# Building the slot table of a mixture of experts with one-hot products, and streaming the next layer's modulation through router and dispatch

## The reference, cut to what matters

```python
scores = sigmoid(hf @ router_w)                       # 512 x 64
# 4 of 8 groups are kept, then 6 experts of each token
top_w  = take(scores, top_idx); top_w = top_w / sum(top_w) * 2.5
# slot table: every expert owns a run of slots; slot_tok[slot] = token (or none)
out    = swiglu(h_pad[slot_tok], w_gate[e], w_up[e], w_down[e])
routed = sum over the 6 picks of  out * top_w
x      = x + gt2 * (routed + swiglu(hf, shared weights))
# next layer: shift, scale, gate = split(silu(c) @ w_mod + b_mod)
```

## Time and profile before

| | us |
|---|---|
| median of 3 runs | 3005.1 (2999.84 to 3009.19) |
| the profiled execution, its own time | 3002.39 |
| its span in the trace | 3000.7 |
| mean granted TensorE clock | 0.921 of full speed |
| busy: PE, DVE, ACT, POOL | 2539.4, 1357.8, 708.0, 480.1 |

### The profile page before, as it was taken

One profiled execution on the slowest core, in us unless ns is written; L12 is line 12 of the kernel. 1 busy time (PEld: TensorE's weight loads), 2 busy tenths in 40 slices (PEclk: granted clock), 3 DMA queues, 4 the chain that ended last, 5 costly groups with the idle time before them and its releaser, 6 DMA issues. The chain is left out here.

```text
span 3000.7 us, 48849 instructions
## 1 busy us (share of the span) xinstructions
PE 2539.4 (85%) x19595; PEld 1484.2 (49%) x19595; DVE 1357.8 (45%) x2706; ACT 708.0 (24%) x1319; POOL 480.1 (16%) x449
## 2 busy tenths in 40 slices
PE   5999864986599999994679999979998498989988
PEld 2553444945244434331235556458887135545553
DVE  1550646525211111113588795966665562034442
ACT  3111440112011111110324551023333113134441
POOL 0000132300311111110100000022211220025450
PEclk8999877997799999997799999989999799999999
DMA  6110610012599999995715555244443932021001
GB/s 252 45 56 2 225 22 16 7 56 103 164 382 389 391 411 406 393 390 206 255 58 143 161 146 174 109 130 125 133 124 84 351 115 93 6 37 21 15 29 63
DMA packets 329700, 471.39 MB, mean 157 GB/s; under 512 B 152223, under 2 KB 225875, under 8 KB 304773
## 3 DMA queue, kind: packets, MB, share of 16 engines
q1 hardware_dynamic: 302645, 373.86, 36.4%
q10 hardware_dynamic: 12960, 69.21, 5.7%
q0 software_dynamic: 13872, 25.21, 2.3%
HBM read 413.73 MB, written 76.60 MB: 163 GB/s over the span
## 5 line engine op out<-in xcount | busy, mean ns | idle before, releaser
L1871 PE MATMUL psum<-ex_w,hT 128*64 128x512 f32 (+1 forms) x1104 | 333.0, 624 | 24.6 <-DMA ex_w<-in_exp_w_up 22.9
L1871 PEld LDWEIGHTS psum<-ex_w,hT 128*64 128x64 f32 (+1 forms) x1104 | 125.5, 160 | 226.0 <-issue 223.8
L3961 POOL TENSOR_SCALAR mla_pool<-mla_pool,at_stats 128x768 f32<-128x768 f32 x64 | 140.2, 2203 | 254.9 <-DVE at_stats L3979 254.9
L2107 DVE COPY slot_act_t<-psum 128x256 f32<-128x256 f32 x45 | 19.1, 424 | 326.8 <-PE psum L1879 326.8
L557 PE MATMUL psum<-hT,weights 128*128 128x512 f32 x384 | 166.8, 592 | 0.0
L1887 PE MATMUL psum<-ex_w,slot_act_t 128*64 128x512 f32 (+1 forms) x552 | 163.4, 597 | 1.4 <-DVE slot_act_t L2107 1.4
L1856 POOL DMA_INDIRECT scratch_ys<-slot_out,slot_row x45 | 45.5, 1011 | 467.3 <-issue 405.0
L557 PEld LDWEIGHTS psum<-hT,weights 128*128 128x128 f32 x384 | 73.0, 190 | 86.7 <-issue 86.1
L2063 ACT ACTIVATE slot_silu<-psum 128x256 f32<-128x256 f32 x45 | 17.2, 383 | 399.5 <-PE psum L1871 399.5
L3135 PE MATMUL psum<-rs_r_ident,rs_b 64*32 64x96 f32 x1536 | 84.3, 249 | 17.9 <-POOL rs_k_ident L3107 16.5
L3859 PE MATMUL psum<-mla_kT,at_qT 128*128 128x512 f32 (+1 forms) x256 | 93.3, 489 | 2.6 <-DVE at_qT L3971 1.6
(11 more groups left out here) (560 smaller groups left out, 4983.0 us busy)
## 6 DMA issues: line engine op xcount, KB each, us to landing
ex_w<-in_exp_w_gate SPq DMA_DIRECT2D x64, 1024.0 KB, 9.6
ex_w<-in_exp_w_up SPq DMA_DIRECT2D x64, 1024.0 KB, 19.4
ex_w<-in_exp_w_down ACTq DMA_DIRECT2D x60, 1024.0 KB, 10.0
mod_ring<-in_w_mod SPq DMA_DIRECT2D x12, 2048.0 KB, 13.2
scratch_features<-tokens SPq DMA_DIRECT2D x96, 256.0 KB, 3.8
weights<-in_w_in SPq DMA_DIRECT2D x6, 2048.0 KB, 8.1
ex_w<-scratch_ys SPq DMA_DIRECT2D x8, 1536.0 KB, 15.4
ex_w<-in_mod_w SPq DMA_DIRECT2D x6, 2048.0 KB, 20.7
```

Of the source, the lines that this page charges most:

```text
L1871: mm = pe.matmul(bank[at:at + n, :], XT[:, k, at:at + n], W[:, 0:2, k * DE:(k + 1) * DE], start=(k == 0), stop=(k == KD - 1))
L3961: pool.tensor_scalar(Pm[:, q % 2, u, :], Pm[:, q % 2, u, :], st[:, 3, u:u + 1], None, ALU.mult)\
```

## The change

The scatters, the table in HBM, its fill and its read back go. In `dispatch`, after each pick's slot is known, DVE splits the slot into tile and position and writes two one-hot (or scaled one-hot) arrays: `at_pos` (token x 128 positions, for 4 groups of tokens in one instruction) and `at_tile` (token x 69 tiles, with the token's number plus one as value, four instructions). PE multiplies them, 24 products summed in one bank, which is the table already transposed; empty slots are zero. The products stand in PE's list between the two halves of the shared expert's gate and up. The first three gathers of rows move from `all_experts` into `dispatch` behind the index lists; the row buffers are kept over both phases, are used for the token rows first, and are zeroed by POOL.

The modulation stream moves out of `combine`: vectors, bias rows and the first weight chunk are requested in `norm_turn`, chunks 0 to 2 run in `router`, 3 to 5 in `dispatch`. Its ring lies in the buffers of the first resident experts, so these are loaded later, and in the order 0, 2, 1. In `dispatch` DVE now takes the index lists first and after them, in this order, the modulation's columns, the shared expert's two products and the list of further experts. `combine` has no modulation left on any engine. It loads all rows into buffers of their own, in eight loads, each with its semaphore. Semaphores are cleared in ranges.

```diff
 def phase(nc, names, before=None, later=None):
...
-                    for h in handles:
-                        sp.sem_clear(h)
+                for a, b in zip(starts, ends):
+                    sp.sem_clear(range(a, b + 1))
 def load_router(I, sp, R, rw, bias, steps):
...
-    for w in range(3):
-        sp.dma_start(Wb[:, 0, w, :]..., shared[w]...).then_inc(R["sh_in"], 16)
+    sp.dma_start(steps[:, :, :], I["consts"][:, IOTA_COL:ALL_COLS]...).then_inc(R["in_done"], 16)
 class NextMods:
+    def request(self, I, sp):
+        vectors_in(sp, I, self.vec, self.H["vec_in"])
+        self.M.load_bias(sp)
+        self.M.load(sp, 0)
 def router(...):
         @block.sync
+            for n in range(1, RING):
+                M.load(sp, n)
+            for w in range(3):
+                sp.dma_start(Wb[:, 0, w, :]..., shared[w]...).then_inc(S["sh_in"], 16)
+            sp.wait_ge(S["in_done"], 48)
         @block.tensor
...
             mm.then_inc(S["mm_done"], 1)
+            pe.wait_ge(S["mod_silu"], 1)
+            for n in range(RING):
+                M.part(pe, n)
+                if n:
+                    M.sum(pe, n - 1)
+            M.sum(pe, RING - 1)
         @block.scalar
+            act.activation(mods.silu[:, :, 0:2], ..., ACT.Silu).then_inc(S["mod_silu"], 1)
...
+            for n in range(RING):
+                M.evac(act, n)
+                if n:
+                    M.to_row(act, n - 1)
+            M.to_row(act, RING - 1)
 def dispatch(...):
         @block.tensor
             mm.then_inc(S["pos_mm"], 1)
+            M.part(pe, RING)
             pe.wait_ge(S["beaten"], 1)
...
+            for n in range(RING + 1, M.N):
+                M.part(pe, n)
+                M.sum(pe, n - 1)
+            M.sum(pe, M.N - 1)
             for j in range(JX):
...
                 .then_inc(S["order_mm"], 1)
+            pe.wait_ge(S["m_row"], M.N)
+            columns_mm(pe, K, K.bank[0], M.row, (0, D)).then_inc(S["c_mm"], 1)
+            pe.wait_ge(S["sh_in"], 48)
             for m in range(2):
                 if m:
+                    for u in range(TOP_K * JX):
+                        pe.wait_ge(S["picked"], 2 * (u // JX) + 2)
+                        mm = pe.matmul(K.bank[1][:, 0:TILES], at_pos[:, u, :], at_tile[:, u, :],
+                                       start=(u == 0), stop=(u == TOP_K * JX - 1))
+                    mm.then_inc(S["idx_mm"], 1)
...
-            pe.wait_ge(S["back"], 16)
-            pe.transpose(K.bank[1][:, 0:TILES], back[:, :], ...).then_inc(S["idx_mm"], 1)
         @block.scalar
+            M.evac(act, RING)
+            for n in range(RING + 1, M.N):
+                M.evac(act, n)
+                M.to_row(act, n - 1)
+            M.to_row(act, M.N - 1)
             for j in range(JX):
         @block.sync
-            sp.dma_start(table, fill[:, :]).then_inc(S["filled"], 16)
+            for n in range(RING, M.N):
+                M.load(sp, n)
+            sp.wait_ge(S["m_row"], M.N)
+            sp.dma_start(gate_rows, M.row[0:2, 2 * D:3 * D]).then_inc(S["g_stored"], 16)
...
-            for q in range(RESIDENT):
-                load_expert(sp, Wb, buffer_of(q), src(expert_at(sp, order, q)), S["ex_in"])
-            sp.wait_ge(S["scattered"], 1)
-            sp.dma_start(back[:, :], table).then_inc(S["back"], 16)
+            sp.wait_ge(S["c_mm"], 1)
+            sp.wait_ge(S["g_stored"], 16)
+            for q in (0, 2, 1):
+                e = src(expert_at(sp, order, q))
+                if q == 1:
+                    sp.wait_ge(S["idx_mm"], 1)
+                load_expert(sp, Wb, buffer_of(q), e, S["ex_in"])
         @block.gpsimd
-            for k in range(TOP_K):
-                for j in range(JX):
...
-                    pool.indirect_dma_start(
-                        out=slot_tokens, out_offset=..., in_=K.const[:, TOKEN_COL + u:TOKEN_COL + u + 1], ...)
...
+            for n in range(RING, M.N):
+                M.add_bias_of(pool, n)
+            for n in range(2):
+                pool.wait_ge(S[f"h_st{n}"], 32)
+            pool.memset(Hg[:, :, :], 0.0).then_inc(S["zeroed"], 1)
+            pool.wait_ge(S["idx_out"], 1)
+            for t in range(RING_H):
+                gather_rows(pool, Hg[:, t, :], idx[:, first_column(t):...], h_rows, S[f"got{t}"])
         @block.vector
+            dve.wait_ge(S["m_part"], M.N)
             for k in range(TOP_K):
...
-                step.put(dve.tensor_reduce(to_f[:, k, :], pr[:, :, :], AX.X, ALU.add))
+                step(dve.tensor_reduce(to_f[:, k, :], pr[:, :, :], AX.X, ALU.add))
+                step.put(dve.tensor_scalar(tile0[:, k, :], to_f[:, k, :], ...))
...
+                step.put(dve.tensor_scalar(tile0[:, k, :], tile0[:, k, :], WHOLE, None, ALU.add))
...
+                step(dve.tensor_scalar(tile0[:, k, :], tile0[:, k, :], -WHOLE, float(SLOTS), ALU.add, ALU.mult))
+                step(dve.tensor_tensor(in_tile[:, k, :], to_f[:, k, :], tile0[:, k, :], ALU.subtract))
+                dve.tensor_tensor(at_pos[:, k * JX:(k + 1) * JX, :], ..., ALU.is_equal).then_inc(S["picked"], 1)
+                for j in range(JX):
+                    ins = dve.tensor_scalar(at_tile[:, k * JX + j, :], steps[:, 1, 0:TILES], tile0[:, k, j:j + 1],
+                                            number[:, k, j:j + 1], ALU.is_equal, ALU.mult)
+                ins.then_inc(S["picked"], 1)
...
+            columns_out(dve, K.bank[0], ..., next_mods[:, 1, :, :], next_mods[:, 0, :, :], S["c_out"])
+            for n in range(2):
...
+                dve.tensor_tensor(aT[:, n, :], sg[:, :], K.bank[up_bank[n][1]][:, :], ALU.mult).then_inc(S["act_done"], 1)
...
 def all_experts(...):
-            pool.wait_ge(S["zeroed"], 1)
-            for t in range(RING_H):
-                gather(t)
-            dve.memset(Hg[:, :, :], 0.0).then_inc(S["zeroed"], 1)
 def combine(...):
-            vectors_in(sp, I, vec, S["vec_in"])
-            load(0)
-            load(1)
...
-            for n in range(3):
-                M.load(sp, n)
-            M.load_bias(sp)
...
+            for n, (j, h) in enumerate(LOADS):
+                k = slice(h * TOP_K // 2, (h + 1) * TOP_K // 2)
+                sp.dma_start(rows[:, j, k, :], ys...).then_inc(S[f"in{n}"], 16)
+                if n == 1:
+                    sp.dma_start(gb[:, :], I["g_final"].partition_broadcast(P)).then_inc(S["g_in"], 16)
+            sp.dma_start(K.X[:, 0:JC, :], I["ctx_2"][0]...).then_inc(S["ctx_in"], 16)
...
-            M.evac(act, 0)
-            for n in range(M.N):
...
+            for j in range(JX):
+                lengths(j)
+                if j:
+                    next_lengths(j - 1)
```

More of the change, by code:

```diff
@@ L52, in phase @@
 @contextmanager
-def phase(nc, names, before=None):
+def phase(nc, names, before=None, later=None):
     with ExitStack() as own:
         by_name = {n: own.enter_context(nc.semaphore(n)) for n in names.split()}
-        signals = {**by_name, **(before or {})}
-        handles = list(signals.values())
+        cleared = {**by_name, **(before or {})}
+        handles = list(cleared.values())
+        signals = {**cleared, **(later or {})}
         with nc.Block(no_gpsimd_drain=True) as block:
@@ L65, in _ @@
                 nums = sorted(h.num for h in handles)
-                if nums[-1] - nums[0] + 1 == len(nums):
-                    sp.sem_clear(range(nums[0], nums[-1] + 1))
-                else:
-                    for h in handles:
-                        sp.sem_clear(h)
+                starts = [n for n in nums if n - 1 not in nums]
+                ends = [n for n in nums if n + 1 not in nums]
+                for a, b in zip(starts, ends):
+                    sp.sem_clear(range(a, b + 1))
 class Chain:
@@ L156, in constants @@
     out[:, LANE_COL:FUTURE_COL] = np.triu(np.ones((RC, RC)), 1).reshape(1, -1)
+    out[:, IOTA_COL:IOTA_COL + P] = np.arange(P)
+    out[:, IOTA_COL + P:ALL_COLS] = np.arange(P) * SLOTS
     e = np.arange(RC + 1)[None, :]
@@ L2413, in mixture @@
         Wb = sb("ex_w", [P, AT_ONCE, 3, KD * DE])
+        Hg, steps = sb("slot_rows", [P, RING_H, D]), sb("slot_steps", [P, 2, P])
+        G = held(nc, c, GATHERED)
         spare = K.hT[:, :, :].rearrange("p k t -> p (k t)")
@@ L2417, in mixture, with ahead @@
             rw, bias = sb("rt_w", [P, KD, NE], F32, c2), sb("rt_bias", [P, NE], F32, c2)
-            R = held(nc, c2, "in_done sh_in")
+            R = held(nc, c2, "in_done")
+            mods = NextMods(K, I, Wb, held(nc, c, NextMods.SEMS))
+            def ahead(sp):
+                load_router(I, sp, R, rw, bias, steps)
+                mods.request(I, sp)
             norm_turn(K, range(JC, NT), K.mods[:, 1, 0, :, :], K.mods[:, 1, 1, :, :], K.inv,
-                      ahead=lambda sp: load_router(I, sp, R, rw, bias, Wb, shared))
-            router(K, I, wt, kept, R, rw, bias)
-        dispatch(K, wt, kept, slot_of, w_of, extra, order, h_rows, slot_tokens, idx, to_row, Wb, src, acc)
```

(6 more changed lines are left out.)

231 lines of the change are left out of this document (104 added, 127 removed).

## The result

The changed kernel takes 2964.1 us (median of 4 runs, 2958.97 to 2970.11); the kernel before took 3005.1 beside it. The ratio is 0.9863, 95% interval 0.9846 to 0.988.

What follows compares the result with a forecast made beforehand. PE and DMA were taken to bound the experts, waits router, dispatch and combine; +16.2 up to the first pass and -31.9 in combine made -15.7, 2986.7 or 2989.4 by base, forecast 2988 us, range 2974 to 3001.

Steps and rivals of the forecast that it cites:

- Fewer clears of semaphores: At changes of phase: clears hidden or gone, below 4.43 us, between 0 and -1, taken as 0.
- Dispatch, first pass +16.2 us: Router and dispatch up to the first expert pass: PE turns the first rows at 831.1 instead of 814.85.
- Ranks to order: In dispatch: ranks and chunk 3's part end at 747.4, chunks 4 and 5 at 758.6, order at 764.9.
- Picks: DVE in dispatch: six picks of 4.4 us each, 2.17 before, ending at 791.6; bounds 3.5 and 5.5 a pick.
- Sum: Whole kernel: +16.2 - 31.9 = -15.7 us; bounds picks -0 to +5, products -3 to +2, combine's tail -2 to +4, cold starts -5 to 0.
- Combine: Combine stage: 57.5 us instead of 89.4, so -31.9, bound by DVE, its first sum 6 us in.
- the stall that I had named: In dispatch: DVE is through with its slots at 755 and stands until 764.9 for the order.
- Late lists: Rival, 18%: dispatch's chunk loads land 5 us later and each pick takes 5.5, so +5 and +4, 2997 us.
- a load-bound combine: Rival, 8%: DVE waits about 3 us at each combine tile, 12 us of the gain go, 3000 us.
- a PE stuck at the low level: Rival, 6%: PE in dispatch stays at the low clock, about +44 us, 3032 us.
- The clock holds: Rival, 12%: parts, both halves and products run at the high clock, 11.4 us less, about 2977 us.
- a product like these doesn't raise the clock: PE in dispatch: the 24 products leave the clock low; 8 us taken, between 4.9 at high clock and 9.7.

Runs made afterwards that it cites:

- experiment 1: Kernel before with range clears (283 fewer): 2991.03 us, ratio 0.9952; changed kernel with single clears: 2988.59 us; kernel before with single clears doubled: 3026.7 us.
- experiment 3: The changed kernel with POOL's zeroing of the gather block moved behind the index lists, away from DVE's picks: 2961.59 us, ratio 0.9854.
- experiment 4: The changed kernel with POOL's zeroing behind the index lists and the order product right behind chunk 4's weights part: 2959.03 us, ratio 0.9845.

## Why the prediction was wrong

**The step that failed first: "Fewer clears of semaphores: no row shows one; ... between 0 and -1, I take 0."** Measured: 14 us (ratio 0.9952 for this edit alone), 0.056 to 0.058 per clear in the two changes of phase that were compared. Two errors are in that sentence. I bounded the sum over the whole program by one change of phase, although the diff is in the helper that all of them use; 283 clears fall away in 13 phases. And there were rows: the 328 single clears stand in the trace of the kernel before, 0.06 to 0.07 us apart (experiment 1), from which 17 to 20 us for 283 would have been the estimate. Without them, I had cited 4.43 us for one change of phase and never set it beside others of the same trace. The change into the scan (67 clears) takes 6.82 and that into the norm (27) takes 2.72; that slope is 4.1 / 40 = 0.1 a clear, nearly twice what was measured but the right order, and would have given a bound of 28 us where I put 1.

**The step that failed second: "Dispatch, first pass +16.2 us".** By the absolute marks it was 822.80 - 814.85 = +7.95, so the terms of this stretch were too high by 8.3 together:
- Router's end 730.2 forecast, 727.3 measured (ACT's last row): 0.8 of it is an earlier start, 1.6 the first part at 4.83 instead of 6.46.
- Ranks to order: 764.9 forecast for the order cast, 758.76 measured. Chunk 3's part took 5.12 for 6.46. The wait for its weights, 2.29, was larger than my 0.7, but the products ahead of it were done sooner than the 10.0 that I had taken over from the kernel before: that duration held a wait of 0.73 and products at the low clock, 7.15 us for what took 6.10 here.
- Columns 3.73 for 4.61. First half 15.70 for 16.7, second 16.48 for 16.7: cold starts are there, as I said, but each smaller than 2.8 where the clock was partly up.
- Picks 4.33 for 4.4, right. The second was 2.0 longer beside POOL's memset, which I had named and priced at nothing; experiment 3 shows it on the path.
- Index product 789.3 for 794.2, because all ahead of it was sooner. Products 0.115 each, near the fast end of my bounds (0.10 to 0.20).
- Change of phase: from ACT's last copy at 821.10 to the first turn 1.7 us, where I carried over 4.43. With 34 clears more, in the changed kernel with single clears, it is 3.6; so 1.9 of the 2.7 are again the clears, and no run parts the rest.

Two slips stand in the sums besides. The bounds listed under "Sum" add up to -10 and +11, which is 2978 to 2999 and not 2980 to 2996, and six picks of 4.4 from 764.9 end at 791.3, not 791.6. Neither would have moved the forecast to what was measured.

**Combine was right:** 57.3 for 57.5, the first sum 6.1 us in for 6.2, a tile 11.8 for 11.8. The expert stage kept its length. The waits for table and rows went without a rest, and what took their place was the stall that I had named, DVE for the order, 7.1 us for 10.

**The rivals.** Late lists, a load-bound combine and a PE stuck at the low level didn't come. "The clock holds" came in part: the first 32 instructions of the products ran near the high level, but the halves still began slow, and the router's products took 12.66 for 64, 0.198 each, as before. So of the two voices that I weighed, the row and the Trainium skill, "TensorE: Matmul & The Clock Gate", section "Part 1: The HAM clock gate" (slow by default, released by sustained activity), the row was right for the router (its products stood in a stretch at 0.50, 1.2 GHz, in experiment 4's trace too, 700 to 712) and the rule for the products behind the first half: in experiment 4, where PE worked on without a pause, the granted clock was 1.00 through all 48 of them. My reading "a product like these doesn't raise the clock" had no bearing there, since the clock was already up and needed only to be kept. The other rule, the Trainium skill, "SBUF — State Buffer", section "Who interferes with whom" (POOL and a DVE operation in a two-port mode take their shared port in turns, the second blocked), this case's trace bears out: 0.17 and 0.42 us became 2.52 and 2.44 beside a POOL memset of 2.66, the second of the two queued behind the first.

Had I priced the clears at the 14 us of experiment 1 and left all else, the forecast would have been 2974; the 6 us of the way to the first turn that are not clears bring it to 2968, 4 above the measured median.

## What to carry to other kernels

When a diff touches a helper that every phase uses, multiply its cost by the phases before calling it small, and read the changes of phase of the whole trace side by side: their lengths against the number of clears give the price. When work is moved between phases, copy no duration that contains a wait or a cold start; cut it into its parts first. And a stall on PE inside dense work can cost its own length and then the slower work behind it (4.6 us cost 8.4 here, 2.9 cost 4.8), so what PE waits for should stand as early as possible in the list of the engine that makes it.

## What was not expected of the hardware

- One single clear of a semaphore on SP costs 0.056 to 0.058 us at a change of phase, and 283 of them 14 us in a program of 3000.
- The same 32 small products of the columns left the granted clock at 1.00 in one kernel and let it fall to 0.94, then 0.83, in another whose list is the same from there on (3.73 and 4.42 us; the half behind them 14.00 and 16.63). The first is the exception: behind these products the first half took 15.6 to 16.6 in every other trace in which it stands behind them.
- The rwkv heads, which no edit touches, took 461.1 us in one trace (stream alone) and 470.6 in another (changed, single clears). The granted clock in that stage goes with it: 0.97 at 461, 0.95 at 470. A single profiled execution can thus hide or feign 9 us, and for effects of 2 to 8 us only marks close to the edit decide.
